# A two-block network in float32 on one core: 224 tokens of an expert layer computed densely, 32 by gathered rows

## What is computed

```python
sc, pos = lax.top_k(cand, PEER_TOPK)
eidx = jnp.take_along_axis(cidx, pos, axis=-1)
g = jax.nn.softmax(sc, axis=-1)
u = jnp.take(expert_u, eidx, axis=0)
a = jnp.einsum('thkd,td->thk', u, hc).astype(jnp.float32)
act = (jax.nn.gelu(a, approximate=False) * g).astype(hc.dtype)
vv = jnp.take(expert_v, eidx, axis=0)
return jnp.einsum('thk,thkd->td', act, vv)
```

## Time and profile before

| | |
|---|---|
| median of 3 executions | 1415.27 us (1412.72 to 1416.08) |
| the profiled execution | 1414.68 us |
| its span in the profile | 1412.6 us |
| TensorE's mean granted clock | 0.993 |
| PE, PEld busy | 98%, 96% |
| DVE, ACT, POOL busy | 71%, 49%, 28% |

### The profile page before, as it was taken

The page is one execution under the profiler, slowest core; times in us unless marked ns, Lnnn a source line. Parts: engine busy times, 40 slices in busy tenths (PEclk is TensorE's granted clock), DMA queues, the critical chain, the costliest instruction groups (busy, mean ns, idle before and its releaser), DMA issues.

```text
span 1412.6 us, 28033 instructions
## 1 busy us (share of the span) xinstructions
PE 1383.5 (98%) x11486; PEld 1357.0 (96%) x11486; DVE 1006.8 (71%) x2242; ACT 692.0 (49%) x1188; POOL 392.5 (28%) x185
## 2 busy tenths in 40 slices
PE   6999999999999999999999999999999999999998
PEld 6989899999999999999999999999999899999988
DVE  3573525859998898999966666776667954788743
ACT  5563446544454444444443333333345766656653
POOL 3744467678600000000000000000000553674332
PEclk9998999999999999999999999999999999999999
DMA  8433345555565444444455766556655534555553
GB/s 284 141 103 105 105 133 180 169 165 182 180 204 168 150 149 150 150 149 150 150 174 187 239 184 190 190 185 192 186 188 180 163 122 137 177 165 179 174 171 104
DMA packets 65095, 234.99 MB, mean 166 GB/s; under 512 B 7228, under 2 KB 7612, under 8 KB 64968
## 3 DMA queue, kind: packets, MB, share of 16 engines
q1 hardware_dynamic: 64968, 233.20, 51.8%
HBM read 232.13 MB, written 1.05 MB: 165 GB/s over the span
## 4 chain that ended last, share of the span: by engine, by line
PE 85%; DVE 9%; ACT 4%; issue 1%; DMA 0%; POOL 0%; SPq 0%; DVEq 0%; ACTq 0%
PE PS L551 84%; ACT SPL L991 2%; DVE SPL L1372 2%; DVE ub L2026 2%; DVE ub L2022 1%; DVE ub L2019 1%; PE PS L673 1%; DMA RAW<-in_dense 0%; DVE HF L1389 0%; DVE RS L1384 0%; DVE HS L1394 0%; DVE sb L1953 0%; ACT HS L1016 0%; DVE PS L1415 0%; DVE cosr L1915 0%
## 5 line engine op out<-in xcount | busy, mean ns | idle before, releaser
L991 ACT ACTIVATE SPL<-RAW 128x1024 fp32r<-128x1024 f32 x432 | 456.4, 1058 | 565.3 <-PE PS L551 561.9
L2049 POOL TENSOR_TENSOR SPL<-RAW,SPL 128x1024 fp32r<-128x1024 f32 x149 | 361.0, 2426 | 1000.8 <-ACT SPL L991 1000.7
L551 PE MATMUL PS<-HS,SPL 128*128 128x256 f32 x4656 | 572.8, 282 | 12.8 <-DVE SPL L1372 11.9
L551 PEld LDWEIGHTS PS<-HS,SPL 128*128 128x128 f32 x4656 | 554.2, 188 | 17.2 <-issue 15.7
L1372 DVE TENSOR_TENSOR SPL<-RAW,SPL 128x1024 fp32r<-128x1024 f32 x283 | 352.0, 1245 | 224.2 <-ACT SPL L991 223.1
L551 PE MATMUL PS<-asp,SPL 128*128 128x256 f32 x3072 | 358.7, 279 | 0.0
L551 PEld LDWEIGHTS PS<-asp,SPL 128*128 128x128 f32 x3072 | 358.5, 188 | 0.1
L551 PE MATMUL PS<-HXb,SPL 128*128 128x256 f32 x720 | 89.6, 285 | 1.9 <-DVE SPL L1372 1.3
L551 PEld LDWEIGHTS PS<-HXb,SPL 128*128 128x128 f32 x720 | 87.1, 189 | 3.1 <-DVE SPL L1372 2.1
L1750 DVE TENSOR_SCALAR oh<-CC,T3f 128x128 f32<-128x128 f32 x256 | 87.6, 342 | 0.0
L1749 DVE TENSOR_SCALAR oh<-CC,T3f 128x128 f32<-128x128 f32 x256 | 72.0, 281 | 0.0
(11 more groups left out here) (253 smaller groups left out, 1175.6 us busy)
## 6 DMA issues: line engine op xcount, KB each, us to landing
RAW<-in_dense SPq DMA_DIRECT2D x176, 512.0 KB, 3.6
RAW<-in_eu SPq DMA_DIRECT2D x128, 512.0 KB, 3.5
RAW<-in_ev SPq DMA_DIRECT2D x128, 512.0 KB, 4.2
bias<-in_nab SPq DMA_DIRECT2D x2, 768.0 KB, 8.3
XT<-in_xT SPq DMA_DIRECT2D x4, 256.0 KB, 5.5
out_y<-HF SPq DMA_DIRECT2D x4, 256.0 KB, 2.4
c<-in_c SPq DMA_DIRECT2D x1, 960.0 KB, 6.9
c<-in_c SPq DMA_DIRECT2D x1, 512.0 KB, 5.4
```

Source lines behind the costliest of these rows:

```text
L551: return e.matmul(out, l, r, start=start, stop=stop, skip_group_check=skip)
L991: e.activation(spl(n)[0], raw(n), ACT.Copy).then_inc(*up("act_high", ("hi", n)))
L2049: e.tensor_tensor(lo, raw(n), hi.bitcast(f32), ALU.subtract).then_inc(*up("pool_low", ("lo", n)))
```

## The change

The expert layer is computed densely for tokens 0 to 223 (W = 224); the last 32 tokens (TG) take another way.

- Every rounded matmul of U and V streams 224 columns instead of 256: 3072 of U, 3072 of V.
- 56 gate steps instead of 64; the same 76 slots of U are spread over them.
- GpSimd makes the low parts of U's slots 50 to 127, which VectorE made.
- ScalarE makes the high parts of the activations in the V steps (a copy of 128 x 224); VectorE keeps the low parts.
- For the 32 tokens VectorE puts the indices and gates of the chosen experts in token columns (`chosen`, eight small operations on 32 x 32). GpSimd issues for each token an indirect DMA of 128 rows of U and one of 128 rows of V, 512 KB each, into two buffers each: the first pair beside U step 60, the other 31 pairs from V step 0 on. Each waits until the token two before is done with its buffer.
- Token j belongs to V step 107 j / 31, rounded down (0, 3, 6, 10, ... 107). VectorE multiplies U's rows by the token's input and sums (`dot`, 128 x 1024); one step later ScalarE applies gelu and the gate to the 128 values; two steps later VectorE adds V's rows times these to yrow, 128 x 1024 over all 32 tokens. The 128 partitions are the token's 4 groups of 32 experts in turn.
- For the inputs by token, ScalarE copies four times the 32 tokens at U step 6, TensorE turns them with 8 plain matmuls beside U steps 8 and 9, and ScalarE stores the result.
- At the end of V, TensorE folds yrow into the accumulators with 8 plain matmuls of 32 columns.

```diff
 def low_on_dve(n):
+    if EXPERT + ROUTED + 2 <= n < EXPERT + NE:
+        return False
     if EXPERT + LISTED <= n < AFTER + 4:
         return True
...
-                        t = mm3(ps[:, 0:256], (hi[:, c, :], lo[:, c, :]), rhs_h(c), c == 0, c == 7)
+                        t = mm3(ps[:, 0:W], (hi[:, c, :], lo[:, c, :]), (HS[:, 0, c, 0:W], HS[:, 1, c, 0:W]), c == 0, c == 7)
...
+                elif what == "a":
+                    w.wait_ge(*at("gated4", W // 4 - 1))
+                    w.wait_ge(*at("ev", "u", i))
+                    if i >= 4:
+                        w.wait_ge(*at("v", i - 4))
+                    e.activation(asp[i % 4][:, 0:W], GB[:, i, :], ACT.Copy).then_inc(*up("act_part", ("ahi", i)))
...
+            def chosen():
+                for g in range(GROUPS):
+                    c = slice(TG * g, TG * g + TG)
+                    r = slice(TG * g, TG * g + TG)
+                    e.scalar_tensor_tensor(erow[r, 0:TG], sel[128 - TG:128, 1, 1, c], 128.0, sel[128 - TG:128, 0, 1, c],
+                                           ALU.mult, ALU.add).then_inc(*up("dve_pick", ("erow",)))
+                    e.tensor_copy(grow[r, :], sel[128 - TG:128, 2, 1, c]).then_inc(*up("dve_pick", ("grow",)))
...
+                    if i in beside:
+                        j = beside[i]
+                        w.wait_ge(*at("urow", j))
+                        w.wait_ge(*at("ev", "xrow", 1))
+                        u_ = urow[j % 2]
+                        e.scalar_tensor_tensor(u_, u_, 1.0, xrow, ALU.mult, ALU.mult,
+                                               accum_out=hrow[:, j:j + 1]).then_inc(*up("dve_row", ("dot", j)))
+                    if i - 2 in beside:
+                        j = beside[i - 2]
+                        w.wait_ge(*at("vrow", j))
+                        w.wait_ge(*at("hrow", j))
...
+                            t = e.scalar_tensor_tensor(yrow, vrow[j % 2], hrow[:, j:j + 1], yrow, ALU.mult, ALU.add)
...
+            def gather(j):
+                rows_ = bass.IndirectOffsetOnAxis(ap=erow[:, j:j + 1], axis=0)
+                if j >= 2:
+                    w.wait_ge(*at("dot", j - 2))
+                e.indirect_dma_start(urow[j % 2], None, A["er"], rows_).then_inc(*up(f"urow{j % 2}", ("urow", j), by=16))
+                if j >= 2:
+                    w.wait_ge(*at("yrow", j - 2))
+                e.indirect_dma_start(vrow[j % 2], None, A["ev"].rearrange("a b c -> (a b) c"), rows_).then_inc(
+                    *up(f"vrow{j % 2}", ("vrow", j), by=16))
```

More of the change, by code:

```diff
@@ L11 @@
 NE = 128
+TG = 32
+W = T - TG
+GROUPS = 128 // TG
 NRAW = 4
@@ L33 @@
 _at = 0
-for _n, _w in (("ident", 128), ("iota", 128), ("permd", 128), ("permr", 128)):
+for _n, _w in (("ident", 128), ("iota", 128), ("permd", 128), ("permr", 128), ("fold", TG)):
     C0[_n] = (_at, _w)
@@ L95, in peer_steps @@
         u += 1
-    for m in range(T // 4):
+    for m in range(W // 4):
         yield "g", m
-        while (u - ROUTED) * (T // 4) < (m + 1) * BESIDE:
+        while (u - ROUTED) * (W // 4) < (m + 1) * BESIDE:
             yield "u", u
@@ L114, in peer_steps, with gather_slots @@
         yield "v", j
+def gather_slots():
+    return {j * 107 // (TG - 1): j for j in range(TG)}
 def first_steps():
@@ L276, in build @@
         top_.take("gap0", 8)
+        ar = Arena()
+        rows1 = ar.take("rows1", 2048)
+        ar.close()
         HSt = top_.take("HS", 4096, f32r)
@@ L333, in build @@
         T3f = ex.take("T3f", 768).rearrange("p (b t) -> p b t", b=3)
+        rows = ex.take("rows", 2048)
+        xrow, yrow = rows[:, 0:1024], rows[:, 1024:2048]
+        copies = yrow.rearrange("p (c m) -> p c m", c=8)
+        urow = [ex.take("urow", 1024), rows1[:, 0:1024]]
+        vrow = [ex.take("vrow", 1024), rows1[:, 1024:2048]]
+        hrow, grow, erow = RS[:, 0:TG], RS[:, TG:2 * TG], RS[:, 2 * TG:3 * TG].bitcast(u32)
         ar = Arena()
-        GB = ar.take("GB", NE * 256).rearrange("p (i t) -> p i t", t=256)
+        GB = ar.take("GB", NE * W).rearrange("p (i t) -> p i t", t=W)
         ar.close()
         ar = Arena()
-        ar.take("first", 58 * 256)
+        ar.take("before", ROUTED * W)
         keysT = ar.take("keysT", 256).rearrange("p (a n) -> p a n", a=2)
@@ L842, in pe_program @@
                         vs, parts_v = [i - 1, i], last_v + parts_v
+                        w.wait_ge(*at("yrow", TG - 1))
+                        for c in range(8):
+                            o = bank((0, 1, 4, 7)[c // 2])[:, (c % 2) * 256 + W:(c % 2) * 256 + 256]
+                            mm(o, yrow[:, c * 128:c * 128 + 128], con("fold"), False, False, True)
                     for c in range(8):
@@ L1802, in angles @@
                     yield
-            routing, turning = route(), angles()
+            routing, turning, beside = route(), angles(), gather_slots()
             for _ in range(4):
@@ L1809, in dve_program @@
                     run(routing)
+                    w.wait_ge(*at("selected"))
+                    chosen()
                     for a in range(2):
@@ L2077, in pool_program @@
                     cur[0] += 1
+                if (what, i) == ("u", ROUTED + 12):
+                    w.wait_ge(*at("erow"))
+                    gather(0)
+                if (what, i) == ("v", 0):
+                    w.wait_ge(*at("used", EXPERT + NE - 1))
+                    for j in range(1, TG):
+                        gather(j)
             run(walk(cur, 8, 2, split, nothing))
```

60 lines of the change are left out of this document (45 added, 15 removed).

## The result

The changed kernel takes **1421.19 us** (median of 6 executions, 1419.46 to 1424.29), the kernel before 1414.09 (6 executions, 1412.27 to 1416.75). The ratio is 1.0051, 95% interval 1.0036 to 1.0066: slower by half a per cent. The profiled execution is the longest of the six, 1424.29 us with a span of 1422.1.

The account below looks back on a forecast made before the run. TensorE was taken to set the time, with VectorE nearly full in the first two stages. The terms -15.9 + 1.8 + 24.4 - 1 - 0.6 + 1 gave +9.7 on 1414.7, 1424 us, range 1378 to 1475.

Parts of the forecast that it names:

- V steps: 128 V steps on TensorE, each 0.124 us shorter at 2.676 us: -15.9 us.
- fold: Folding yrow into the accumulators at V's end adds 8 plain matmuls, 16 records of 0.1115 us: +1.8 us.
- gate steps: VectorE's one-hot tiles wait for GpSimd's low parts, so this stage grows from 267.0 to 291.4 us: +24.4.
- before the gates: Stage before the gate steps: faster TensorE wins at most VectorE's 3.9 us idle, `chosen` returns 1.6: -1, between -4 and +2.
- five slots: The five U slots after the last gate run with narrower matmuls: -0.6 us.
- first gather: The first indirect DMA sits in GpSimd's queue before low parts: +1 us, up to +8.
- The width: Matmuls of 224 instead of 256 columns take 111.5 ns, the floor set by loading 128 columns of weights, instead of 116.7.
- the streaming pace: Rival: streamed columns alone set a matmul's time, 102.1 ns; V steps -44.8, total 1394 us; chance 0.10.
- no gain: Rival: 224 columns still take 116.7 ns a matmul and the gate steps' +24 stands alone, 1440 us; chance 0.11.
- the plain pace: Rival: rounded matmuls under 256 columns fall to plain matmuls' speed, 400 ns at 224 columns, over 3100 us; chance 0.04.
- the rival by which the tiles don't wait: One-hot tiles aren't held by GpSimd, TensorE sets the gate steps: -16.5 instead of +24.4, 1383 us; chance 0.17.
- My rival: V steps: one indirect DMA takes GpSimd over 4.6 us, VectorE waits for `urow`; at 6 us each +87, 1511 us; chance 0.13.

Follow-up runs that it names:

- experiment 4: Kernel before, V-step matmuls narrowed to 240, 224, 192, 128 and 64 columns in some stretches; single execution 1445 us; 2.68 us a step at 224 to 128 columns.
- Experiment 2: Kernel before, only with GpSimd taking the low parts of U's slots in the gate steps: 1459.75 us, ratio 1.0321.
- experiment 1: Changed kernel with the low parts of U's slots in the gate steps back on VectorE: 1384.87 us, ratio 0.9787.
- experiment 3: Changed kernel, GpSimd keeping the low parts, but the one-hot tiles read the column numbers from PSUM: 1384.33 us, ratio 0.9782.
- experiment 5: The kernel of experiment 1 with the 32 tokens' row operations in 54 V steps instead of 108: 1441.83 us, ratio 1.0199.
- experiment 8: The kernel of experiment 5 with U's gather of the next token queued before V's gather of this one: 1409.52 us, ratio 0.9956.
- experiment 9: The kernel of experiment 1 with the 32 tokens in 81 V steps instead of 108: 1385.59 us, ratio 0.9793.
- experiment 7: Changed kernel with only every second slot's low part on GpSimd in the gate steps, the others on VectorE: 1390.98 us, ratio 0.9833.
- experiment 6: Kernel before, with the low parts of 112 of V's 128 slots on GpSimd: 1421.84 us, ratio 1.0057.

## Why the prediction came out as it did

The forecast was 1424 us, +9.7 on the profiled execution before; the profiled execution after is 1424.29. It is the longest of its six, so that this agreement is in part luck: from median to median the change costs 7.1 us. Term by term, against the profiled execution before:

| term | predicted | measured |
|---|---|---|
| V steps | -15.9 | 128 x (2.80 - 2.68) = -15.4, and +1.8 for one late load |
| fold | +1.8 | +1.8 (1080.42 to 1082.20) |
| gate steps | +24.4 | 288.6 - 267.1 = +21.5 |
| before the gates | -1 | 438.79 - 441.57 = -2.8 |
| five slots | -0.6 | 13.47 - 14.09 = -0.6 |
| first gather | +1 | lies in the gate steps, below |
| after V | 0 | 334.5 - 331.3 = +3.1 |
| sum | +9.7 | +9.5 on the span |

**The width** was right in kind and size: the weight loads of the earlier trace rows gave 111.5 ns, the V steps have 111.7, and experiment 4 shows the same pace from 224 down to 128 columns. The rivals with the streaming pace (102.1 ns) and with no gain (116.7) are out; so is the plain pace. One load of V is late: ScalarE waits 5.4 us for it at 825.92, and TensorE 1.6 us before VectorE's low part in the page. So the 8 us that I gave a load to land, against 4.2 before, are not always enough beside the gathers.

**The gate steps** were right in their cause. Experiment 2 shows the clause alone doing it, experiment 1 takes it away, and experiment 3 keeps GpSimd's work and takes away only where the tiles read. So the rival by which the tiles don't wait is out, in the changed kernel; it describes experiment 3. The size, +21.5 for +24.4, came out of several errors that partly cancel. The count was wrong: 56 gates have 55 distances between them, 35 with one slot and 20 with two, and behind the last gate only its own 0.89 us belong to the stretch; at my prices that is 289.9 us, 1.5 less than my 291.4. Also, the period of 4.48 took GpSimd's end as 7.15 where my own 0.89 + 2.68 + 1.1 + 2.40 give 7.07, a period of 4.44. Then the prices. I gave a gate with two slots the serial sum, 6.61 us; from the 56 starts (438.79 to 726.42) the 19 such behind the first took 6.35 in the mean, only 0.10 over TensorE's own 6.25 in experiment 1. The tiles are made two steps ahead, so a gate's sum need not be met within that gate: in 19 gates -5. The 35 of one slot took 4.55 against my 4.48: +2.5. The first interval is 7.79 us, 1.4 over the others of two slots; TensorE waits 1.21 of it for a low part that VectorE makes behind a held tile (2.52 us long, from 439.19). I had no term for that: +1.2. With the count's -1.5 these make the -2.8 from 291.4 to 288.6. The first gather, which I put at +1, shows too: GpSimd's two issues (490.76 to 493.27 us) stand in front of a low part, and that gate takes 5.10 us, the longest of one slot, 0.5 over their mean.

**The gathers** cost nothing here, as predicted, but the bound that I gave was the wrong one. "Up to 4.6 us each on GpSimd it costs nothing" counted the queue's time; the rows above show 0.93 to 1.98. What sets the limit is the trip of three tokens (5.8 to 6.2 us a token by the estimate, 6.6 measured in experiment 5), split into two of two tokens by experiment 8. The change asks 9.25 us, experiment 9 6.9, and both cost next to nothing. My rival's place was right (VectorE in front of `urow`, V's low parts behind it), its point was not: it begins at a spacing between 4.6 and 6.9 us a token.

**Before the gates and after V** the terms were too small. In all seven profiled executions with the change's 224 columns (the change, experiments 1, 3, 5, 7, 8 and 9) the first gate starts at 436.9 to 438.8 us, in the four of the kernel before and its variants (experiments 2, 4 and 6) at 439.6 to 441.6. The means are 2.8 us apart, where I had put -1. The stretch after V, to which I gave no term, takes 332.9 to 336.6 us in the seven and 331.3 to 332.8 in the four, with the same 2556 matmuls, 3.0 us apart in the means. In the change's profiled execution the granted clock is 0.96 for the 40 us from 1127.6 on, where the kernel before has 1.00; experiment 2 has this 0.96 too, and why it comes more often in the seven is not shown. Row by row of the table the forecast missed by +2.3 (V steps), -2.9, -1.8, -1.0 (the gather's row, which the gate steps hold) and +3.1 us, and that these cancel to a few tenths is luck.

**Where the expected gain went.** Eight gate steps fewer and the narrower slots are worth 267.1 - 251.0 = 16.1 us in the gate steps, and 358.5 - 345.0 = 13.5 in the V steps (experiment 1). The first was not only lost but reversed, by 37.5 us of tiles that stand behind GpSimd. The version that beats both kernels is the change without its third part, or with it and the tiles' input in PSUM: 1385 and 1384 us.

## What to carry to other kernels

Before moving work to an idle GpSimd, list what VectorE does at that time and where each operation reads: one that reads one SBUF tensor in the fast form, or two SBUF tensors, is held until GpSimd's ends (tiles and copy up to 2.5 us, the subtraction 2.56), and one that has a tensor in PSUM is not (at most 410 ns a tile in experiment 3). Add the two up one after the other (a held operation at its distance to the next rather than at its duration) and compare the sum with the engine that bounds the stage. And before narrowing a matmul, read the spacing of weight loads with few columns: below it there was nothing to win here, and at 64 columns much to lose. In a queue of gathers, ask what stands in front of each issue and how many tokens a round trip spans.

## What was not expected of the hardware

- **At 64 columns the clock halved.** With PE and PEld busy all the time, the granted clock went from 1.00 to 0.50 within the first steps (980.86 to 991.43), and came back with 256 columns. A step then takes 5.12 us, 213.3 ns a matmul. At 128 columns and more it stayed at 1.00. The Trainium skill's page "TensorE: Matmul & The Clock Gate", section "LDWEIGHTS (loading the stationary operand)", has 106.7 ns for 128 columns of weights: the steps at 1.2 GHz take twice this figure, those at 2.4 GHz (111.7) are 5 ns above it, and the measured 111.7 decides.
- **A held operation costs less than its duration.** In experiment 6 a subtraction and a copy that take 0.42 and 0.29 us alone fit into the 0.39 us between two low parts of GpSimd, and the copy starts 0.20 us after the first of them ends. Why is not shown.
- **TensorE's waits cost more than their length.** In experiment 5 they were 37.0 us, and the lower granted clock behind them cost another 19.4; in experiment 8 14.4 and 11.6.
- **A gather of 512 KB by GpSimd takes 7.3 to 7.9 us to land**, where a plain load of V of the same size took 4.3 in the same run.
